# Normed input 256 bytes and MLP activation 16 bytes past the weights' offset modulo 512, in a 1-core network kernel

## What is computed

```python
# first block, layer i; kind is i % 3
h = rmsnorm(x, norm_mix_g[i])
x = x + mixer(h)                       # gated recurrence (1280 wide), spatial gate, or short convolution
x = x + square(relu(rmsnorm(x, norm_mlp_g[i]) @ w1[i])) @ w2[i]
# second block
proj = rmsnorm(h, norm_mix_g) @ w_in   # then rwkv7 scan, dilated attention, gates
h = h + merged @ w_out
h = h + cross_attention(rmsnorm(h, norm_x_g), rmsnorm(mem, norm_mem_g))
h = h + square(relu(rmsnorm(h, norm_ffn_g) @ ffn_w1)) @ ffn_w2
return rmsnorm(h, norm_final_g)
```

## Time and profile before

| what | value |
|---|---|
| runs | 3473.33 and 3468.74 us |
| span of the profiled execution | 3463.6 us (its own time is not given apart) |
| TensorE busy | 3370.7 us, 97% |
| TensorE weight loads busy | 2754.4 us, 80% |
| VectorE busy | 1764.5 us, 51% |
| ScalarE busy | 1162.7 us, 34% |
| GpSimd busy | 467.8 us, 14% |
| mean granted TensorE clock | 0.992 |
| DMA | 329.56 MB, mean 95 GB/s |

### The profile page before, as it was taken

How to read it: one execution, slowest core, us unless ns; L and a number is a source line. 1 busy time by engine, 2 the same in 40 slices (tenths; PEclk the granted TensorE clock), 3 DMA queues, 4 the chain that set the end, 5 groups by cost and what they waited for, 6 DMA issues and landing times. The chain is left out here.

```text
span 3463.6 us, 51738 instructions
## 1 busy us (share of the span) xinstructions
PE 3370.7 (97%) x21556; PEld 2754.4 (80%) x21556; DVE 1764.5 (51%) x1954; ACT 1162.7 (34%) x1455; POOL 467.8 (14%) x417
## 2 busy tenths in 40 slices
PE   7999999999999999999999999999998889999998
PEld 5588888888888888887588888788776878878887
DVE  7764343454344554345765253655686555555342
ACT  3532123432222232222532123334563543332122
POOL 2011011020011021011011012000141221111011
PEclk9999999999999999999999999999999999999999
DMA  4233333233322233233233323343332122313232
GB/s 131 72 105 99 97 97 97 86 97 97 97 97 86 96 101 105 87 103 109 69 98 97 98 96 109 102 133 115 100 96 91 41 65 86 122 61 100 94 98 72
DMA packets 313270, 329.56 MB, mean 95 GB/s; under 512 B 22786, under 2 KB 304389, under 8 KB 312581
## 3 DMA queue, kind: packets, MB, share of 16 engines
q1 hardware_dynamic: 306325, 303.39, 27.6%
q0 software_dynamic: 4464, 19.40, 1.7%
q10 hardware_dynamic: 2304, 4.20, 0.3%
HBM read 312.28 MB, written 14.68 MB: 94 GB/s over the span
## 5 line engine op out<-in xcount | busy, mean ns | idle before, releaser
L501 PE MATMUL ps<-xh,wh 128*128 128x512 f32 x2360 | 930.6, 394 | 10.5 <-DVE wl L438 10.5
L501 PE MATMUL ps<-xh,wl 128*128 128x512 f32 x2360 | 920.1, 390 | 0.0
L501 PE MATMUL ps<-xl,wh 128*128 128x512 f32 x2360 | 919.7, 390 | 0.0
L438 DVE TENSOR_TENSOR wl<-raw,wh 128x2048 fp32r<-128x2048 f32 (+2 forms) x281 | 634.0, 2256 | 423.0 <-ACT wh L433 422.3
L433 ACT ACTIVATE wh<-raw 128x2048 fp32r<-128x2048 f32 (+1 forms) x284 | 526.9, 1855 | 668.7 <-PE ps L501 641.8
L501 PEld LDWEIGHTS ps<-xh,wh 128*128 128x128 f32 x2360 | 444.1, 188 | 115.9 <-issue 22.8
L501 PEld LDWEIGHTS ps<-xl,wh 128*128 128x128 f32 x2360 | 444.1, 188 | 95.2 <-issue 4.3
L501 PEld LDWEIGHTS ps<-xh,wl 128*128 128x128 f32 x2360 | 443.7, 188 | 93.1
L501 PE MATMUL ps<-hh,wh 128*128 128x512 f32 x1280 | 498.5, 389 | 1.2 <-DVE wl L438 0.9
L501 PE MATMUL ps<-hh,wl 128*128 128x512 f32 x1280 | 498.0, 389 | 0.0
L501 PE MATMUL ps<-hl,wh 128*128 128x512 f32 x1280 | 498.0, 389 | 0.0
(11 more groups left out here) (426 smaller groups left out, 3680.2 us busy)
## 6 DMA issues: line engine op xcount, KB each, us to landing
raw<-in_mlp_w SPq DMA_DIRECT2D x128, 1024.0 KB, 5.4
raw<-in_ffn_w SPq DMA_DIRECT2D x32, 1024.0 KB, 5.2
raw<-in_w_in SPq DMA_DIRECT2D x31, 1024.0 KB, 5.3
raw<-in_a_w_in SPq DMA_DIRECT2D x20, 1024.0 KB, 5.1
raw<-in_c_w_in SPq DMA_DIRECT2D x12, 1024.0 KB, 5.1
raw<-in_a_w_out SPq DMA_DIRECT2D x16, 640.0 KB, 4.0
raw<-in_b_w_in SPq DMA_DIRECT2D x8, 1024.0 KB, 5.7
raw<-in_xa_wkv SPq DMA_DIRECT2D x8, 1024.0 KB, 6.0
```

The source lines that it names most:

```text
L438: nc.vector.tensor_tensor(wl[:, p.slot(su), 0:n], raw[:, p.slot(su), 0:n], wh[:, p.slot(su), 0:n], ALU.subtract).then_inc(lower, 1)
L501: last = nc.tensor.matmul(banks[mt][:, 0:st.n], stat_, ops[oi][at_, kk, 0:st.n], start=k == 0 and su == 0 and n_ == 0, stop=k == kb - 1 an ...
```

## The change

xh and xl begin 256 bytes later, hh and hl 16 bytes past their former residue. A name `xspace` reserves the longer stretch for x. hh and hl become views into stretches of 16 bytes more, the second of which begins at 32.5 KiB. Because the arena base is moved up to the weights' residue again, all of the arena lies 512 bytes higher, and ident to hf and the parameters 256 bytes higher. To make room fo moves from 64 to 65 KiB, and PCs moves into unused columns of prm3. In byte numbers xh is now at 82336 and xl at 98720 (residue 416), hh at 132784 and hl at 166064 (residue 176); wh and wl stay (residue 160), as do the residues of yh, yl, rh, rl, oh, ol, mh, ml, gdh, gdl, yah and yal.

```diff
@@ -117,8 +117,10 @@
     wl = pers("wl", [P, 2, 8, 256], F32R)
     x = pers("x", [P, ND, T])
     XH_AT = used[0]
-    xh = pers("xh", [P, ND, T], F32R)
-    xl = pers("xl", [P, ND, T], F32R)
+    X_OFF, H_OFF = 256, 16
+    xspace = pers("xspace", [P, 2 * ND * T + X_OFF // 4], F32R)
+    xh = nc.alloc_sbuf_tensor_at("xh", [P, ND, T], F32R, offset=XH_AT + X_OFF)
+    xl = nc.alloc_sbuf_tensor_at("xl", [P, ND, T], F32R, offset=XH_AT + ND * T * 4 + X_OFF)
     ident = pers("ident", [P, P])
@@ -146,8 +148,8 @@
-    hh = at("hh", 0, [P, 16, T], F32R)
-    hl = at("hl", 32, [P, 16, T], F32R)
+    h_space = [at(n_, k_, [P, H_OFF // 4 + 16 * T], F32R) for n_, k_ in (("hh", 0), ("hl", 32.5))]
+    hh, hl = (v[:, H_OFF // 4:].rearrange("p (k t) -> p k t", t=T) for v in h_space)
@@ -199,7 +201,7 @@
-    PCs = at("PCs", 94.25, [P, NC, NH2])
+    PCs = prm[3][:, 64:P].rearrange("p (c q) -> p c q", c=NC)
@@ -243,7 +245,7 @@
-    fo = at("fo", 64, [P, ND, T])
+    fo = at("fo", 65, [P, ND, T])
```

## The result

The changed kernel takes 3487.23 us (median of two runs, 3487.01 and 3487.44) against 3471.03 us: a ratio of 1.0058, with a 95% interval of 1.004 to 1.0076. It is slower by 16 us, and 1.000 lies outside the interval. The forecast was 3471.

What follows compares the result with a forecast made beforehand. The prediction took TensorE, busy for 97% of the span, to bound the kernel through its split matmuls. All terms were taken as 0, so the forecast stayed at 3471 us, with a range of 3345 to 3550.

Steps and rivals of the forecast that it cites:

- The unit and the count: Split matmuls on TensorE: 226.7 ns from start to start; 11,592 read a shifted operand, filling 2,557 us, 74% of the span.
- x at +256, a term of 0: 7,752 matmuls that read x parts: taken as 0, within bounds of -96 and +103 us.
- h parts at +16, a term of 0: 3,840 matmuls that stream the hidden activation: taken as 0 for the same reason as x, bounds -48 and +51 us.
- the late load in the earlier trace: A weight load starting 0.12 us into the running matmul; intervals stayed 0.22 and 0.24 us, read as evidence against a residue effect.
- The rival on the other side: Split matmuls: the shift spoils the settling at 226.7 ns; 231.4 ns for all costs 54 us, giving 3525; chance 26%.
- the sign that I named: In the chain of waits after the change, the longest L501 piece divided by its matmul count.
- my three readings: Of that quotient: 226.7 ns means no effect, 214 to 220 the shared residue, 231 or more the spoiled settling.
- The shared residue as the cause: Split matmuls: stream and load sharing a residue modulo 512 makes the excess; full gain 144 us, giving 3327; chance 34%.
- the excess of 12.4 ns: Split matmuls: the interval of 226.7 ns exceeds the 214.3 ns that streaming 512 columns twice costs; 144 us over 11,592.
- Constants, arena, register operation, PCs, fo: Moved constants and arena, DVE's added register operation, PCs in prm3 and fo at 65 KiB: each taken as 0.
- The Trainium skill: TensorE: streaming operand and weight load have independent read ports, so no relative offset could matter; its gap formula gives 215.8 ns.
- the forecast's own range of 3460 to 3481: Whole kernel: the narrower range around the forecast of 3471 us, the case of an offset without effect; chance 40%.

## Why the prediction was wrong

- *The unit and the count.* Right: 226.7 ns from start to start, 3,840 h matmuls, TensorE alone on the path. The cost per matmul could be multiplied out to the microsecond.
- *x at +256, a term of 0.* Right, 354 and 354 in the window, but by luck: it rested on the same argument as the term for h, and 256 happens to be the period of the pattern, which nothing in the prediction knew.
- *h parts at +16, a term of 0.* This is the step that failed: "I take 0 for the same reason", within bounds of -48 and +51. It measured +19.2 us. The reason was the late load in the earlier trace rows: another moment, the same excess. But that row speaks of y, which is level with the weights and on a multiple of 32; it varies when the two reads meet, not where they begin. I let a change of time stand for a change of address. The runs show that they are not the same: at one address the interval runs through 224 to 236 ns and settles at 226.67 in ten matmuls, at another it never does.
- *The rival on the other side was the mechanism.* "That point may not exist, and the stream stays in what the earlier trace rows shows as a transient", at a mean of 231.4 ns; measured 231.65. It was priced for all 11,592 matmuls, 54 us, and struck 3,840. That +16 could cost and +256 not, I did not consider: where a rival priced one operand by itself, it was x for a loss and either for a gain, never a loss of h alone. So the sign that I named, the longest piece divided by its count, gives 296.71 / 1296 = 228.9 ns and fits none of my three readings, because it mixes x at 226.7 with h at 231.7.
- *The shared residue as the cause.* Refuted: of the 15 other offsets in steps of 16 within the period, and 4 and 8, none has an interval below that of 0. Being level isn't the reason for the excess of 12.4 ns but the best that was found.
- *Constants, arena, register operation, PCs, fo.* Right at 0, by the run with h alone put back.
- *The Trainium skill.* By its page "TensorE: Matmul & The Clock Gate", section "Step-by-step: what each phase is for", the streaming read and the weight load don't disturb each other, so no relative offset could cost. The measurement decides against that for this type: moving the weights by 16 bytes and leaving r and o where they were took those from 226.67 to 233.33, and moving h by 32 bytes cost 6.7 ns a matmul, moving both by 32 nothing.

The range of 3345 to 3550 held the time, but the forecast's own range of 3460 to 3481 did not. That the loss stayed at 16 us is no merit of the sum: x at +16 cost 34 us when it was tried.

That the loss comes from where the stream lies to the weights is shown. That the excess of 12.4 ns comes from the same two reads is still an argument. No run here had a stream without a load, and which parts of memory stand behind 256 and 32 isn't shown.

## What to carry to other kernels

Where matmuls of a type that is read at the full rate fill the time, read the interval from start to start in a settled stretch, and place streamed and loaded operands level modulo 256 with starts at a multiple of 32 until measured otherwise; a misplaced operand mostly cost 2 to 11 ns in 227 here. Whether an interval settles shows in ten rows of the order of time. An effect of addresses can't be read from a stretch in which only the moment differs: move the address, and use the stages of one program as so many trials.

## What the runs showed of the hardware

- *Intervals fall on a grid.* At the full clock, the settled interval is 226.67 or 233.33 ns, 34 or 35 times 6.667. Where it doesn't settle on one value, turns of several add up to the grid: four at 231.67 make 139 steps, two at 230.0 make 69, three at 228.89 make 103, three at 231.11 make 104. For +4, and for +64 and +128 in the run that used them throughout, no such short turn was found in the last 150 matmuls. Starts of settled stretches all over the kernel before, hundreds of microseconds apart, agree modulo 6.667 ns apart from a steady drift of 1.6 ns in a millisecond. A reading that fits, and isn't shown: the interval depends on where in a step a matmul starts, and a stretch settles when it comes to a point that leads back to itself.
- *Plain fp32 and the lower clock have no excess.* 429 ns for 512 columns and 0.43 us at 1.2 GHz are twice 214, without the excess.
- *The exchanged roles behave otherwise.* In line 478, where x slices are loaded and 256 weight columns stream, an offset of x lowered the interval: 119.9 ns on average at 0 (intervals under 130 ns, which leaves out waits and the lower clock), 118.6 at +16, 117.7 at +48, 115.7 at +8 and 115.4 at +64. With 672 of them that is 3 us at best, too little to be measured here.
- *Start addresses.* The Trainium skill's page "SBUF — State Buffer", section "Operand start alignment", lets an operand start at any multiple of its element size and adds that its runs timed nothing. Here h at +4 cost 237.37 - 226.67 = 10.7 ns a matmul, and x at +8 cost 6.7 or 5.7.
